# RWKV-7 scan on one Trainium2 core: the right-hand side summed in PSUM and multiplied by the inverse once

## The reference, cut to what matters

```
def step(state, inp):                        # state is [head, v, k]
    r_t, w_t, k_t, v_t, a_t, b_t = inp
    sa = einsum('bhvk,bhk->bhv', state, a_t)
    state = state * w_t + sa (x) b_t + v_t (x) k_t
    y_t = einsum('bhvk,bhk->bhv', state, r_t)
```

## Time and profile before

| | |
|---|---|
| median of 3 runs | 1509.52 us (1507.62 to 1509.68) |
| the profiled execution | 1508.86 us, its span 1507.1 us |
| PE busy in the span | 1475.0 us (98%) |
| DVE, ACT, POOL busy | 1043.1 (69%), 683.4 (45%), 132.5 us (9%) |
| granted TensorE clock | 1.0 of full speed |
| the scan | from about 596 to 691 us |

### The profile page before, as it was taken

One profiled execution on the slowest core, in us unless ns is written; L12 is line 12 of the kernel. 1 busy time (PEld: TensorE's weight loads), 2 busy tenths in 40 slices (PEclk: granted clock), 3 DMA queues, 4 the chain that ended last, 5 costly groups with the idle time before them and its releaser, 6 DMA issues.

```text
span 1507.1 us, 24905 instructions
## 1 busy us (share of the span) xinstructions
PE 1475.0 (98%) x9685; PEld 1218.0 (81%) x9685; DVE 1043.1 (69%) x1626; ACT 683.4 (45%) x1232; POOL 132.5 (9%) x163
## 2 busy tenths in 40 slices
PE   6999999999999999999999999999999999999998
PEld 5987888777777888887788888888888888888887
DVE  6566764578687582679865489777777757777785
ACT  7555664244433213756313246444444433333453
POOL 1013320000010001364000020000000000000000
PEclk9999999999999999999999999999999999999999
DMA  5031002722222536204446115444443699889754
GB/s 193 15 80 43 16 16 63 225 68 71 83 73 62 170 126 150 90 4 137 130 163 240 54 58 175 152 153 154 150 149 136 229 332 326 277 281 301 270 180 151
DMA packets 181115, 216.53 MB, mean 144 GB/s; under 512 B 28789, under 2 KB 115186, under 8 KB 180242
## 3 DMA queue, kind: packets, MB, share of 16 engines
q1 hardware_dynamic: 180942, 215.11, 43.5%
q10 hardware_dynamic: 68, 0.02, 0.0%
HBM read 156.20 MB, written 56.92 MB: 141 GB/s over the span
## 4 chain that ended last, share of the span: by engine, by line
PE 84%; DVE 8%; ACT 4%; issue 2%; DMA 2%; SPq 0%; ACTq 0%; DVEq 0%
PE bank L3113 20%; PE bank L3511 20%; PE bank L3575 13%; PE bank L3476 5%; PE bank L3417 4%; PE bank L3011 3%; PE bank L3023 2%; PE bank L3038 2%; PE bank L2900 2%; PE bank L2967 2%; PE bank L3048 2%; DVE down_raw L2715 1%; DVE hacc L2755 1%; PE bank L3606 1%; PE bank L2931 1%
## 5 line engine op out<-in xcount | busy, mean ns | idle before, releaser
L3113 PE MATMUL bank<-uT_hi,w_hi 128*128 128x512 f32 x432 | 170.8, 395 | 0.0
L3113 PE MATMUL bank<-uT_hi,w_lo 128*128 128x512 f32 x432 | 168.2, 389 | 0.0
L3113 PE MATMUL bank<-uT_lo,w_hi 128*128 128x512 f32 x432 | 168.2, 389 | 0.0
L3575 PE MATMUL bank<-mg_lo,mg_hi 128*128 128x512 f32 x576 | 134.8, 390 | 0.6 <-DVE mg_hi L2722 0.6
L3575 PEld LDWEIGHTS bank<-mg_lo,mg_hi 128*128 128x128 f32 x576 | 107.9, 188 | 24.2 <-DVE mg_hi L2722 1.9
L3575 PE MATMUL bank<-yh,mg_lo 128*128 128x512 f32 x384 | 118.2, 389 | 0.0
L1419 ACT ACTIVATE zbuf<-bank 128x512 f32<-128x512 f32 x54 | 32.2, 599 | 173.2 <-PE bank L3113 168.9
L1786 ACT ACTIVATE f<-f 128x512 f32<-128x512 f32 x64 | 40.5, 632 | 131.6 <-DVE f L2680 69.7
L3113 PEld LDWEIGHTS bank<-uT_hi,w_hi 128*128 128x128 f32 x432 | 81.1, 188 | 21.7 <-issue 5.2
L3113 PEld LDWEIGHTS bank<-uT_hi,w_lo 128*128 128x128 f32 x432 | 81.1, 188 | 17.4 <-issue 1.0
L3113 PEld LDWEIGHTS bank<-uT_lo,w_hi 128*128 128x128 f32 x432 | 81.1, 188 | 17.1
(11 more groups left out here) (510 smaller groups left out, 3759.2 us busy)
## 6 DMA issues: line engine op xcount, KB each, us to landing
down_raw<-in_w_ff_down SPq DMA_DIRECT2D x80, 512.0 KB, 4.9
down_raw<-f_spill SPq DMA_DIRECT2D x56, 512.0 KB, 4.8
f_spill<-x SPq DMA_DIRECT2D x80, 256.0 KB, 2.9
w_raw<-in_w_in SPq DMA_DIRECT2D x28, 512.0 KB, 4.2
sgate<-gate_spill SPq DMA_DIRECT2D x16, 512.0 KB, 4.2
up_a<-in_w_ff_up SPq DMA_DIRECT2D x16, 512.0 KB, 4.9
up_b<-in_w_ff_up SPq DMA_DIRECT2D x16, 512.0 KB, 4.1
f_spill<-f SPq DMA_DIRECT2D x32, 256.0 KB, 2.6
```

The source lines that it names most:

```text
L3113: ins = nc.tensor.matmul(ps[2 * slot + g][:], st[:, slot, k, :], mv[:, k, g * HALF:(g + 1) * HALF], start=(k == 0 and m == 0), stop=(k == ...
L3575: ins = nc.tensor.matmul(ps[4 * (q % 2) + t][:], st, mv_, start=(start and w == 0 and m == 0), stop=(stop and w == 1 and m == 2))
```

## The change

The masked matrix by v (`mv`) stays in PSUM, in banks 3 (even heads) and 4 (odd heads), and the product of a with the state is added to it there (`right_side`); VectorE copies the even heads and ScalarE the odd heads (`x_evac`), T is multiplied into the sum once (`u_product`), and the two engines copy the result into `vu` (`u_copy`). `solve_mv`, `solve_a`, the third group of transposes and the tiles `an` and `tat` are gone, with their copies. The orders on PE, VectorE and ScalarE are new: among others `y_product` is split, `y_scale` stands ahead of the second `state_update`, and in the last iteration ScalarE's `o_high(1)`, `round_late_sigmoids` and `o_high(2)` come behind `u_copy(15)`. `transpose_y` of the first four pairs uses bank 0. SP's loads wait for other counts: that of `lnw` for the first `right_side`, that of o (`oraw`) for the third, that of `w_o` for the last `u_product`. The rest is renaming of semaphores, counts of three instead of four naturals, and placement (`sgt` at 87 KB). Cut to its core:

```diff
--- before.py
+++ after.py
@@ -837,7 +836,7 @@
                 sp.wait_ge(s_gs[0], 16 * stored_gates(NW - 1 - (NW - 1) % 2))
                 sp.wait_ge(s_gs[1], 16 * stored_gates(NW - 1 - NW % 2))
                 load_v(NT // 2, NT)
-                sp.wait_ge(s_tam, 1)
+                sp.wait_ge(s_xm, 1)
                 sp.dma_start(lnw[:], a["ln_w"][0:1, :].partition_broadcast(P)).then_inc(s_ln, 16)
                 sp.dma_start(lnb[:], a["ln_b"][0:1, :].partition_broadcast(P)).then_inc(s_ln, 16)
...
@@ -867,7 +866,7 @@
                 sp.wait_ge(s_ym, NT - 2)
                 sp.wait_ge(s_bv, NT - 2)
                 sp.dma_start(sg_in[:], g_dram[:]).then_inc(s_sgl, 16)
-                sp.wait_ge(s_twm, 2 * NT)
+                sp.wait_ge(s_um, 2 * NT)
                 for b in range(2):
                     load_wo(b, b)
...
@@ -1519,38 +1518,30 @@
+                def x_evac(n):
+                    r = own(n % 2)
+                    act.wait_ge(s_xm, n + 1)
+                    nc.scalar.activation(wv[r, 1, :], ps[4][r, 0:256], ACT.Copy).then_inc(s_xea, 1)
+                def u_copy(n):
+                    i, m = n // 2, n % 2
+                    act.wait_ge(s_um, n + 1)
+                    u = vu[other(m), (i + 1) % 3, m, :].rearrange("p (c h v) -> p c h v", h=2, v=RH)[:, :, 1, :]
+                    nc.scalar.activation(u, ps[6][other(m), 0:256].rearrange("p (c v) -> p c v", v=RH), ACT.Copy).then_inc(s_ua2, 1)
...
@@ -1593,32 +1584,32 @@
                 nat_evac(0, 0)
                 for i in range(-1, NT):
                     j = i + 1
-                    if 2 <= i < NT - 1:
+                    if i >= 0:
+                        x_evac(2 * i)
+                    if i >= 2:
                         square_y(i - 2)
+                    if i >= 0:
+                        u_copy(2 * i)
+                    if i == NT - 1:
+                        o_high(0)
                     if j < NT:
                         nat_evac(j, 1)
-                        w_evac(j, 0)
+                    if i >= 0:
+                        x_evac(2 * i + 1)
+                    if i >= 2:
+                        root_y(i - 2)
+                    if i >= 0:
+                        u_copy(2 * i + 1)
+                    if j < NT:
+                        nat_evac(j, 3)
+                    if i >= 3:
+                        evac_y(i - 3)
                     if i == NT - 1:
-                        o_high(0)
-                        square_y(i - 2)
                         o_high(1)
                         round_late_sigmoids()
                         o_high(2)
-                    if j < NT:
-                        nat_evac(j, 2)
-                    if i >= 3:
-                        evac_y(i - 3)
-                    if j < NT:
-                        tw_evac(j, 0)
-                    if i >= 2:
-                        root_y(i - 2)
-                    if j < NT:
-                        nat_evac(j, 3)
-                        w_evac(j, 1)
-                        tat_evac(j)
-                        tw_evac(j, 1)
-                        if j + 1 < NT:
-                            nat_evac(j + 1, 0)
+                    if j + 1 < NT:
+                        nat_evac(j + 1, 0)
                     if i == 0:
                         round_gup(0)
                         round_gup(1)
@@ -2375,13 +2366,18 @@
-                def u_add(n):
+                def x_evac(n):
+                    r = own(n % 2)
+                    dve.wait_ge(s_xm, n + 1)
+                    nc.vector.tensor_copy(wv[r, 0, :], ps[3][r, 0:256]).then_inc(s_xed, 1)
+
+                def u_copy(n):
                     i, m = n // 2, n % 2
                     dve.wait_ge(s_um, n + 1)
-                    dve.wait_ge(s_tw, 2 * (i + 1))
-                    u = vu[other(m), (i + 1) % 3, m, :].rearrange("p (c h v) -> p h c v", h=2, v=RH)
-                    both = banks[other(m), 5 * 512:7 * 512].rearrange("p (h q) -> p h q", h=2)[:, :, 0:256]
-                    nc.vector.tensor_tensor(u, both.rearrange("p h (c v) -> p h c v", v=RH), u, ALU.add).then_inc(s_us, 1)
+                    if i >= 3:
+                        dve.wait_ge(s_ym, i - 2)
+                    u = vu[other(m), (i + 1) % 3, m, :].rearrange("p (c h v) -> p c h v", h=2, v=RH)[:, :, 0, :]
+                    nc.vector.tensor_copy(u, ps[5][other(m), 0:256].rearrange("p (c v) -> p c v", v=RH)).then_inc(s_us, 1)
...
@@ -2442,25 +2438,27 @@
                 for i in range(-1, NT):
                     j = i + 1
                     if i >= 0:
-                        u_add(2 * i)
+                        x_evac(2 * i)
+                        u_copy(2 * i)
                     if j < NT:
                         mask(j, 0)
                     if i >= 0:
                         state_update(2 * i)
+                    if i >= 2:
+                        y_var(i - 2)
+                    if i >= 0:
+                        x_evac(2 * i + 1)
                     if j < NT:
                         mask(j, 1)
+                    if i >= 0:
+                        u_copy(2 * i + 1)
                     if i == NT - 1:
                         o_low(0)
-                    if i >= 0:
-                        u_add(2 * i + 1)
-                    if i >= 2:
-                        y_var(i - 2)
-                    if j < NT and i >= 0:
-                        state_update(2 * i + 1)
-                    if i == NT - 1:
                         o_low(1)
                     if i >= 2:
                         y_scale(i - 2)
+                    if j < NT and i >= 0:
+                        state_update(2 * i + 1)
                     if i == 1:
                         gup_low(0)
                         gup_low(1)
@@ -3219,14 +3217,14 @@
                 def naturals(i, c):
+                    if c == 0 and i >= 5:
+                        pe.wait_ge(s_yt, i - 4)
-                        elif c == 2:
-                            ins = nc.tensor.transpose(ps[0][:, w * P:(w + 1) * P], ar[:, w, 0, tok], ident[:])
...
                 def mv(i, hs):
+                                rows = own(m)
+                                ins = nc.tensor.matmul(ps[3 + h][rows, c * RH:(c + 1) * RH], mq[h][rows, i % 3, c, 0, :],
+                                                       vu[rows, (i + 1) % 3, m, (2 * c + h) * RH:(2 * c + h + 1) * RH],
+                                                       start=(c == 0), stop=False, skip_group_check=True)
+                    ins.then_inc(s_mv, 1)
+
+                def right_side(n):
                     i, m = n // 2, n % 2
-                    pe.wait_ge(s_tat, 2 * (i + 1))
+                    pe.wait_ge(s_mv, 2 * i + 2)
                     pe.wait_ge(s_st, n + 1)
-                    if n:
-                        pe.wait_ge(s_us, n)
+                    tok = slice(i * P + CH * m, i * P + CH * m + CH)
                     for c in range(RC):
                         for h in range(2):
                             rows = slice(64 * h, 64 * h + 64)
-                            ins = nc.tensor.matmul(ps[5 + h][other(m), c * RH:(c + 1) * RH], tat[rows, i % 2, m, c, :],
-                                                   state[rows, n % 2, c, :], start=True, stop=True)
+                            ins = nc.tensor.matmul(ps[3 + h][own(m), c * RH:(c + 1) * RH], ar[rows, c, 0, tok],
+                                                   state[rows, n % 2, c, :], start=False, stop=True, skip_group_check=True)
+                    ins.then_inc(s_xm, 1)
+                def u_product(n):
+                    i, m = n // 2, n % 2
+                    pe.wait_ge(s_xed, n + 1)
+                    pe.wait_ge(s_xea, n + 1)
+                    for c in range(RC):
+                        for h in range(2):
+                            ins = nc.tensor.matmul(ps[5 + h][other(m), c * RH:(c + 1) * RH], tt[own(m), 16 * c + 2 * i + h, :],
+                                                   wv[own(m), h, c * RH:(c + 1) * RH], start=True, stop=True)
                     ins.then_inc(s_um, 1)
...
                 def state_product(n):
+                    pe.wait_ge(s_ua2, n + 1)
...
@@ -3341,12 +3324,10 @@
                 def transpose_y(i):
                     pe.wait_ge(s_pn, i + 1)
                     if i < NT - 4:
-                        pe.wait_ge(s_yc, i + 2)
-                        if i:
-                            pe.wait_ge(s_yt, i)
+                        pe.wait_ge(s_nat, NATS * (i + 5))
...
@@ -3358,37 +3339,41 @@
                 for i in range(-1, NT - 1):
                     j = i + 1
                     if i >= 0:
+                        right_side(2 * i)
+                    products(j, 0)
+                    if i >= 0:
                         u_product(2 * i)
-                    products(j, 0)
                     naturals(j, 1)
                     if i >= 0:
                         state_product(2 * i)
```

(26 more changed lines are left out.)

97 lines of the change are left out of this document (26 added, 71 removed).

## The result

The changed kernel takes 1521.10 us (median of 4 runs, 1519.33 to 1521.71) against 1509.31 for the kernel before (4 runs, 1507.62 to 1509.68): ratio 1.008, 95% interval 1.0068 to 1.0092, 11.8 us slower. The forecast was 1509.5 with a range up to 1514. The profiled execution took 1521.71 (span 1520.0), 12.9 us more than the one before.

The account below looks back on a forecast made before the run. The scan was taken as bound by what PE must issue. Start -2.6, i=0 to 5 -0.8, i=6 +0.25 and tail +3.2 sum to +0.05 us, so 1509.5 us, range 1503 to 1514 (forecast case's own 1506.5 to 1512.5).

Parts of the forecast that it names:

- What goes, start: Start of the scan: PE drops one group of transposes, two solve_mv and solve_a, -2.6 us.
- The walk: One scan iteration followed through the in-order queues: steady period 11.1 us instead of 11.57, 0.9 of 1.34 saved becomes waiting.
- Rival C: Scan, slower: copy plus handover costs 0.1 us more, period 11.7, seven add 4.2, total 1513.7; chance 0.22.
- adds two right_side at 0.62: PE per pair: 0.58, two 1.24 and 0.76 go, two groups at 0.62 come; net -1.34 of 11.57 us.
- the rule against the change: New u_product on one tile: weight loads uncovered, 2.1 us instead of 0.62, +1.5 for each of 16, +24.
- Rival D: u_product: weight loads are exposed, total 1533 us; chance 0.03.
- mv at 0.82: PE in the walked iteration: both mv, after transpose_y and before naturals(j+1,0), take 0.82 us.
- Steady period: Scan, i=3 to 5: 11.1 us per iteration instead of 11.57, 33.3 together.
- One of the signs: Middle of the scan: PE busy falls from 10.88 to about 10.3 of 11 us.
- i=1 and i=2: Scan: ScalarE's g_up roundings delay x_evac and so u_product; i=1 takes 12.0 us, i=2 12.05.
- i=6: Scan: POOL's additions slow y_scale, now ahead of state_update(13), delaying right_side(14); 11.4 us against 11.15, +0.25.
- Tail: Last pair: sigmoid roundings behind u_copy(15), gate products at 12.3 us against 7.56, +4.7; later waits absorb part, 3.2 stay.

Follow-up runs that it names:

- two column groups: Changed kernel with only u_product's odd heads put into the chunk's own half of PSUM's partitions, so products alternate between two tiles: 1516.55 us, ratio 1.0051.
- the tail's order: Gate sigmoids rounded before late o_high, y_scale(5) before o_low(1); on changed kernel with ScalarE reordered, two-tile u_product, square_y moved: 1508.29 us; on changed kernel alone: 1519.77.

## Why the prediction was wrong

The waits in front of PE came where and for whom they were forecast, and nearly as long; the sizes of two groups of products were not, and one cost was not in the list. By the steps of the prediction:

- **What goes, start.** -2.6 forecast, 602.58-605.07 = -2.5 measured. Right.
- **The walk.** The releaser of every wait was named right: 0.43 forecast in front of `u_product(2i)` for ScalarE's wv, 0.50 measured; 0.29 for the mask, 0.26 measured. The copies took VectorE 0.42, as taken. Rival C's late handovers did not come, but for at most the 0.2 us per period that are left over below; its sign did.
- **The step that failed: "adds two right_side at 0.62 (same form as the present u_product)", and with it the decision "I follow the row" under the rule against the change.** The new `u_product` was put at `state_product`'s 0.62 because that one never changes its rows either. It does change its columns. With neither changed it is 1.04 to 1.08: +0.43, for 16 of them 6.9 us. Two column groups gave the 0.43 back, twice per period. Rival D named the right group, with a price of 1.5 that is more than three times the measured one, and with another mechanism: it took one whole weight load of 0.134 us per entry as uncovered, but the loads on one tile lie beside running entries, and the entries start 58 ns apart. What is lost is the second tile's work beside the first's. Why one tile takes an entry each 58 ns and not faster, no run shows. I had bounded the cost (0.62 to 2.1) and kept the lower bound as the value with a chance of 0.97; nothing in the trace excluded a value between, and even a quarter of the way up (16 x 0.37 = 5.9) would have left the range. The argument beside it, that groups which change the tile in both directions run at 0.41 instead of 0.62, does not hold: the 0.62 was read off `solve_mv`, which changes both.
- **The rule of the skill.** The Trainium skill, "TensorE: Matmul & The Clock Gate", Part 3, has weight loads overlap only when the row group differs; the runs agree that the one-tile product is dearer, and don't agree with the rule as it stands: with the same 64 rows throughout and alternating columns the 16 entries took 0.61, and even on one tile the trace has the loads (135 ns) beside running entries.
- **mv at 0.82.** I took it as twice 0.41, the start-to-start time of one half in the earlier trace rows. There the next group, on other tiles, starts while this one still drains. In the changed kernel both halves stand together in front of a group on the whole array: the 32 entries, two side by side every 58 ns, and the 0.15 us behind the last take 1.08: +0.26 in each pair, 2 us in all.
- **Steady period.** 11.1 forecast, 12.49 measured: +0.86 for the two `u_product`s, +0.26 for `mv`, 0.07 for the longer wait; the 0.2 left over is spread over the other groups, none of them more than 0.08 off the walk. One of the signs came true all the same: PE is busy 10.36 of 11.00 us in the middle of the scan (649 to 660), as forecast, because the waits are there; a busy share doesn't tell a shorter period from a longer one.
- **i=1 and i=2.** Both waits behind the roundings came as walked. 12.0 became 15.74 and 12.05 became 14.16: beside the 1.2 to 1.4 of any period, 2.4 and 1.0 more, which are gone in both executions where the clock stayed up. The clock was not thought of: a wait on PE was priced at its length. The single runs put it at 2.0 to 2.4 us of the 11.8, and it comes in some executions, not in all.
- **i=6.** +0.25 forecast, +1.03 measured; with two column groups it is 11.57, so 0.61 are the two `u_product`s (0.86 less what VectorE's state then holds up). The slow step of `y_scale` came (VectorE L1937 beside GpSimd, 1.14 us), and PE waited 0.20 for state 14.
- **Tail.** 12.3 forecast, 13.11 measured, released by ScalarE's sg as said: +0.8, again two `u_product`s ahead of `u_copy(15)`, on which the roundings follow: with two column groups it is 12.35. The 1.5 us of later waits taken up were 1.8. The step is right but for the term above. What was only seen in the runs is that a gain in front of the gate products is waited off behind them, mostly for VectorE: the 1.9 us of the tail's order gave no more than 0.8.

Sum against the forecast, in the profiled execution: 0.1 (start) + 1.5 + 3.7 + 2.1 + 4.2 (i=0 to 5) + 0.8 (i=6) + 0.8 (tail) - 0.3 = 12.9; by cause 6.9 for one-tile products, 2 for `mv`, 3.4 for the clock, 0.6 not assigned. These are sizes on PE's way up to the gate products; taking the first one away gave 4.1 us of the time. The measured best of the variants, 1508.42 and 1508.29, can't be told from the kernel before (ratios 0.9993 and 0.9995, both intervals hold 1): what the change takes from PE, 1.34 us per pair by the forecast and 1.1 with `mv` at its measured size, is given back by the waits of the longer chain and by the tail. What stays open is why one tile takes an entry per 58 ns, and why the clock falls behind the same wait in one execution and not in another.

## What to carry to other kernels

When a group of small products is moved or rewritten, write down for each of its products which rows and which columns of the array it uses; if neither changes from one to the next, don't take the price from a group where one does, and send alternate products to the other 64 partitions of PSUM if the copy behind can read them there. Price a group by how long it takes in front of a group that needs the same tiles, not by the distance of two starts that overlap. In a chain that passes through a copying engine, put that engine's other work behind the copy that TensorE waits for, and count a wait on TensorE as possibly more than its length.

## What the runs showed of the hardware

- 16 entries of 64 x 64 in fp32: 1.04 to 1.08 us on one tile, 0.90 with four products in a row per tile, 0.61 to 0.62 with rows, columns or both alternating. At the full clock a tile took one entry per 58 ns in each of these forms; two tiles ran side by side.
- A PE wait of 1.90 us was followed by 6.8 us at half the clock in one execution and by none in another with a wait of 1.89; waits of about 0.5 us in the last pair were followed by 3.4 us at half the clock in the first and by none in the second. With 11 transposes in place of most of the long wait the clock was 1.00 there in the profiled execution, and the mean 0.998 to 0.999 in all four. The single runs put the price of the low clock at 2.0 to 2.4 us for this kernel.
- ScalarE's copy from one half of the partitions in PSUM to the other half in SBUF costs no more than one within a half. Groups by line of the kernel with two column groups, 600 to 700 us (busy us, mean ns, idle before); L1544 is the copy across halves, L1536 within one, and L3286 is busy 10.9 us where the changed kernel has 18.6 (600 to 720 us) for the same 256 entries:

```profile
L3286 PE MATMUL bank<-wv,tt 64*64 64x64 f32 x256 | 10.9, 223 | 7.3 <-ACT wv L1536 6.2 <-DVE wv L2372 1.1
...
L1544 ACT ACTIVATE vu<-bank 64x256 f32<-64x256 f32 x16 | 6.1, 379 | 12.0 <-PE bank L3286 11.8
...
L1536 ACT ACTIVATE wv<-bank 64x256 f32<-64x256 f32 x16 | 6.1, 378 | 18.9 <-PE bank L3276 18.7
```
